# Shifted starts for the weights' slots and the row tiles of h in an fp32 kernel of two transformer blocks

## What is computed

```
for layer in 0, 1:
    h = modulate(rms_norm(x, g0), sh1, sc1)
    y = gmlp_mixer(h, ...)  if layer == 0  else  nsa_mixer(h, ...)
    x = x + g1 * rms_norm(y, g1n)
    h = modulate(rms_norm(x, g2), sh2, sc2)
    y = square(relu(h @ ff_w_in[layer])) @ ff_w_out[layer]      # 1024 -> 4096 -> 1024
    x = x + g2 * rms_norm(y, g3)
x = x + gt1 * rms_norm(token_mixers(modulate(rms_norm(x)) @ w_in) @ w_out)
u, gate = split(modulate(rms_norm(x)) @ w_up, 2)                # 1024 -> 2 x 2816
x = x + gt2 * rms_norm((silu(dwconv_grid(u)) * gate) @ w_down)
```

## Time and profile before

| | |
|---|---|
| median of 3 runs | 1018.43 us (1018.09 to 1018.6) |
| span of the profiled execution | 1018.0 us |
| TensorE busy | 994.2 us (98%), 6901 matmuls |
| weight loads busy | 877.0 us (86%), beside the matmuls |
| VectorE busy | 802.1 us (79%) |
| ScalarE busy | 539.3 us (53%) |
| from HBM | 239.37 MB, 236 GB/s over the span |

### The profile page before, as it was taken

One profiled execution on the slowest core, in us unless ns is written; L12 is line 12 of the kernel. 1 busy time (PEld: TensorE's weight loads), 2 busy tenths in 40 slices (PEclk: granted clock), 3 DMA queues, 4 the chain that ended last, 5 costly groups with the idle time before them and its releaser, 6 DMA issues.

```text
span 1018.0 us, 16927 instructions
## 1 busy us (share of the span) xinstructions
PE 994.2 (98%) x6901; PEld 877.0 (86%) x6901; DVE 802.1 (79%) x1208; ACT 539.3 (53%) x706; POOL 76.1 (7%) x80
## 2 busy tenths in 40 slices
PE   6999999999999999999999999999999999999997
PEld 3687799989987999887889999988999789999996
DVE  2459799868988987867978878872789799878796
ACT  4354644345446557766545454465764765454544
POOL 0000000000000000000630000000790000000000
PEclk9999999999999999999999999999999999999999
DMA  9999699969997998002999777725434286555511
GB/s 340 386 386 366 227 336 397 334 235 364 328 343 261 281 375 319 2 2 85 393 348 310 269 279 284 250 80 165 126 125 151 99 288 209 195 177 194 179 42 42
DMA packets 130333, 243.60 MB, mean 239 GB/s; under 512 B 6587, under 2 KB 95312, under 8 KB 124112
## 3 DMA queue, kind: packets, MB, share of 16 engines
q1 hardware_dynamic: 125616, 238.77, 66.6%
q10 hardware_dynamic: 4639, 3.76, 1.3%
HBM read 239.37 MB, written 1.05 MB: 236 GB/s over the span
## 4 chain that ended last, share of the span: by engine, by line
PE 85%; DVE 6%; DMA 3%; ACT 2%; issue 2%; SPq 2%; DVEq 0%; ACTq 0%
PE bank L2038 26%; PE bank L1970 13%; PE bank L1971 13%; PE bank L1972 13%; PE bank L2050 3%; DMA raw<-in_a_w_in_dram 1%; SPq L653 1%; DVE wlo L1198 1%; PE bank L2323 1%; DMA raw<-in_b_w_in_dram 1%; PE bank L2349 1%; PE bank L1864 1%; PE bank L2519 1%; DVE hcat L1338 1%; PE bank L2361 1%
## 5 line engine op out<-in xcount | busy, mean ns | idle before, releaser
L1198 DVE TENSOR_TENSOR wlo<-raw,whi 128x2048 fp32r<-128x2048 f32 x143 | 328.6, 2304 | 49.9 <-ACT whi L723 48.1
L723 ACT ACTIVATE whi<-raw 128x2048 fp32r<-128x2048 f32 x144 | 274.1, 1904 | 146.0 <-PE bank L2038 76.1
L1970 PE MATMUL bank<-hcat,whi 128*128 128x256 f32 x1096 | 312.1, 285 | 1.0 <-DVE wlo L1198 0.9
L1971 PE MATMUL bank<-hcat,whi 128*128 128x256 f32 x1096 | 310.1, 283 | 0.0
L1972 PE MATMUL bank<-hcat,wlo 128*128 128x256 f32 x1096 | 310.1, 283 | 0.0
L1970 PEld LDWEIGHTS bank<-hcat,whi 128*128 128x128 f32 x1096 | 210.1, 192 | 7.6 <-issue 3.0
L1971 PEld LDWEIGHTS bank<-hcat,whi 128*128 128x128 f32 x1096 | 210.2, 192 | 1.4
L1972 PEld LDWEIGHTS bank<-hcat,wlo 128*128 128x128 f32 x1096 | 210.1, 192 | 0.0
L1817 DVE SCALAR_TENSOR_TENSOR cvt<-ut,vec,cvt 128x189 f32<-128x189 f32 (+2 forms) x176 | 68.2, 429 | 20.9 <-ACT cvt L1161 18.4
L2038 PE MATMUL bank<-whi,fhi 128*128 128x512 f32 x240 | 75.0, 394 | 0.0
L2038 PE MATMUL bank<-wlo,fhi 128*128 128x512 f32 x240 | 74.1, 390 | 0.0
(11 more groups left out here) (432 smaller groups left out, 1631.1 us busy)
## 6 DMA issues: line engine op xcount, KB each, us to landing
raw<-in_ada_w_dram SPq DMA_DIRECT2D x40, 1024.0 KB, 8.6
raw<-in_ff_w_in_dram SPq DMA_DIRECT2D x32, 1024.0 KB, 7.4
raw<-in_ff_w_out_dram SPq DMA_DIRECT2D x32, 1024.0 KB, 7.1
raw<-in_w_ada_dram SPq DMA_DIRECT2D x24, 1024.0 KB, 6.4
raw<-in_w_up_dram SPq DMA_DIRECT2D x22, 1024.0 KB, 5.1
raw<-in_w_in_dram SPq DMA_DIRECT2D x12, 1024.0 KB, 5.4
raw<-in_w_down_dram SPq DMA_DIRECT2D x11, 1024.0 KB, 4.8
raw<-in_ada_w_dram SPq DMA_DIRECT2D x16, 512.0 KB, 12.1
```

The costliest lines, as they stand in the source:

```text
L723: act.activation(whi[:, m % SPL, 0:w], raw[:, pl.nm[m] % RAW, 0:w], ACT.Copy).then_inc(s_hi, 1)
L1198: dve.tensor_tensor(wlo[:, m % SPL, 0:w], raw[:, pl.nm[m] % RAW, 0:w], whi[:, m % SPL, 0:w], ALU.subtract).then_inc(s_lo, 1)
L1970: pe.matmul(dst, wh[:, kt, n], ah[:, kt, :], start=kt == 0, stop=False)
L1971: pe.matmul(dst, wh[:, kt, n], al[:, kt, :], start=False, stop=False)
```

## The change

The slots of `whi` and `wlo` become 20 values (80 bytes) longer, so they stand 8,272 bytes apart. The row tiles of `hcat` become 8 values (32 bytes) longer, 2,080 bytes apart; within one the high and the low part stay 1,024 bytes apart. The values between are not used. The last region starts at the next multiple of 128 bytes from `whi`, not of 512. By the allocation `wlo` starts 256 bytes later than before, `hcat` 512, `gcat`, the small buffers and the last region 768 (193,664 becomes 194,432). `raw` and `whi` stay. The instructions, their order and their waits are the same on every engine.

```
+W_SHIFT, H_SHIFT = 20, 8
...
-    whi = sb("whi", [P, SPL, CH], F32R)
-    wlo = sb("wlo", [P, SPL, CH], F32R)
+    whi = sb("whi", [P, SPL, CH + W_SHIFT], F32R)
+    wlo = sb("wlo", [P, SPL, CH + W_SHIFT], F32R)
     x = sb("x", [P, 2, D])
-    hcat = sb("hcat", [P, KT, 2, T], F32R)
+    hcat = sb("hcat", [P, KT, 2 * T + H_SHIFT], F32R)[:, :, 0:2 * T].rearrange("p k (a t) -> p k a t", a=2)
...
-    oP = whi_at + (at[0] - whi_at + 511) // 512 * 512
+    oP = whi_at + (at[0] - whi_at + 127) // 128 * 128
```

## The result

The changed kernel takes 1020.63 us (median of 14 runs) where the kernel before takes 1018.63 beside it (14 runs). The ratio of the times is **1.0016, with a 95% interval of 1.0009 to 1.0023**: the forecast gain of 0.9% didn't come, and 0.16% is lost. The profiled execution of after spans 1019.6 us, that of before 1018.0.

The account below looks back on a forecast made before the run. The prediction took TensorE's matmul stream (98% busy) to bound the kernel. 7.2 us less from the 256-column and 1.6 from the 512-column products gave 8.8 us less, 1018.4 to 1009.6 us (0.9% less), range 992 to 1019.5.

Parts of the forecast that it names:

- What bounds the kernel, and that only the two spacings count: Feed-forward blocks: TensorE is filled, so only start-to-start spacings of 120 ns (256 columns) and 227.9 ns (512) set their length.
- rival 4: First feed-forward block: the loads take its gain, 2.4 us are lost, giving 1012.0 us; chance 0.06.
- That the price depends on addresses: Compression products with shifted starts average 117.55 ns, aligned products of the same form 120 ns, so 2.45 ns less.
- Rival 1: All matmuls: addresses don't matter, the compression products' unevenness has another source; same time, 1018.4 us; chance 0.14.
- The 256-column products: Lines 1970 to 1972 in filled stretches: 2,928 matmuls, each 2.45 ns quicker, 7.2 us less.
- The 512-column products: Line 2038: 645 of 968 change phase with slots 1 and 2, each 2.45 ns quicker, 1.6 us less.
- upper bound of 2.0: Line 2038 at worst: the unsettled 230 ns spacing at the start, 2.1 x 968 = 2.0 us more.
- 13 to 14 ns: Loss per 256- or 512-column matmul against one column per cycle, read as the price of a 128-column fp32 weight load.
- Rival 3: Feed-forward blocks: one of three slots meets a bad phase, 10 ns on a third of 2,928, 9.8 us, 1028.2 us; chance 0.12.
- Rival 2: Each matmul falls to the quickest pairs seen, 27.3 us less, 991.1 us; chance 0.16.
- Writes into shifted slots and the region: ScalarE's and VectorE's writes into shifted slots, and the region moved as a whole: nothing at the end, 0 us.
- The signs that were named: Profile after: uneven 256-column steps near 117.5 ns, 24 of line 2038 in 5.40 to 5.47 us, first feed-forward round about 11.06.

Follow-up runs that it names:

- e1: Only the row tiles of `hcat` lengthened by 32 bytes, slots and region as in the kernel before; ratio to before 0.9972.
- e2: Only the slots of `whi` and `wlo` lengthened by 80 bytes, `hcat` and region as in the kernel before; ratio to before 1.0045.
- e3: Nothing lengthened, only the last region starts 256 bytes further than in the kernel before; ratio to before 0.9999.
- e5: Nothing lengthened, the whole of `hcat` moved by 192 bytes against the weights of the kernel before; ratio to before 0.9927, 1012.8 us.
- e9: Against the kernel before, everything from `whi` on moved by 192 bytes and `hcat` another 192; ratio to before 0.9915, 1010.71 us.
- e8: Against the kernel before, everything from `whi` on moved by 192 bytes, all distances as before; ratio to before 1.0001.
- e4: Against the kernel before, slots 64 bytes longer and the second buffers of `chi` and `clo` 16 bytes further; ratio to before 1.0002.
- e7: Against the kernel before, slots 32 bytes longer, `whi` and `wlo` moved by 32 bytes, `hcat` by 96; one execution, 1018.47 us beside 1018.9.
- e10: Against the kernel before, only `hcat` as a whole moved, by 64 bytes; ratio to before 0.996.
- e6: Against the kernel before, slots 32 bytes longer, `whi` and `wlo` moved by 160 bytes, `hcat` by 128; one execution, 1016.72 us beside 1018.9.

## Why the prediction was wrong, step by step

**What bounds the kernel, and that only the two spacings count: right for the feed-forward blocks.** No stage shows a new wait, VectorE's rows and the loads are as before, and the loads took nothing (rival 4): the first block runs at 329 and 330 GB/s.

**That the price depends on addresses: right.** Rival 1 has the time nearly right, but its reason is refuted: e1 gains 0.28% and e2 loses 0.45% by addresses alone. That after looks like "no effect" is a sum of two effects, and that rival 1 comes near is luck.

**The 256-column products: the right sign, the size too large.** The step that failed is "I take their mean, 117.55 ns". After has 118.5 in the first block, 1.3 ns less than before, and 118.3 in the last, 1.6 less (before, 863.40 - 846.42 = 16.98 us with a group of 5.47 left 119.9). With 1.3 for the 640 x 3 = 1,920 up to 810 us and 1.6 for the 336 x 3 = 1,008 behind the earlier trace rows that is 2.5 + 1.6 = 4.1 us instead of 7.2. The mechanism holds and the size was off. The compression products advance by 240 bytes from step to step and these by 32, so they run over other distances, and the table shows 116.7 to 120 by distance; a mean over one set of them isn't the mean over another.

**The 512-column products: the wrong sign.** The step that failed is "I give them the same 2.45 ns, as the price per weight load is the same". Three rounds take 16.61 us in their groups instead of 3 x 5.47 = 16.41, so the 720 of the first two layers (30 groups) lose 10 x 0.20 = 2.0 us; the 248 of the last block (10.3 groups) lose 10.3 x 0.15 = 1.5. That is 3.5 us more where 1.6 less was forecast, and above its upper bound of 2.0: the 230 ns of the earlier trace rows was taken as the worst, and slot 2 has 234. (The outgoing tile of the last block is in slot 2 in every round, so 480 + 248 = 728 of these products change their distance, not two in three, 645. And the two losses that were read as the same, "13 to 14 ns", are 13.3 and 14.6 by the prediction's own rows.) The kernel before has its 512-column products at the best distance of the table, and the prediction didn't ask whether the even 227.9 ns was already good.

The two errors, 3.1 and 5.1 us, are most of the distance between the 8.8 us forecast as a gain and the 1.6 us (0.16%) measured as a loss. By these two terms after would still be 0.6 us ahead.

**The products over `hcat`: a term that the prediction didn't have.** Its sum has `hcat` as the moving operand alone, and ahead of 130 us it counted no more than a possible gain. As stationary operand under 512 columns of weights `hcat` and `gcat` serve 407 steps, which lose 1.9 us: most of the 2 us or so that the two terms leave. Either shift alone does it: in the trace of e1, where only `hcat` is lengthened, these steps lose 1.6 us, and in e2's, where only the slots are, 1.5. So e1's gain would be larger without them. What is left, the 0.9 us in steps of over 0.3 us, is no more than single executions differ by (-1.0 in e3), and stays open.

**Rival 3** had the mechanism and the wrong place: "one of three slots meets such a phase all the time". It does, and two of the three, but in the 512-column products, and the 256-column ones stay under 120, by which the prediction took it as excluded. It was priced at 9.8 us on the wrong products and without the gain of the others beside it; it also stood there as all or nothing, so no case of the prediction held a gain on one form and a loss on the other. **Rival 2**, each matmul at the quickest steps, was far off: no distance of the table is below 116.7. A single tile can come near it (48 steps of 113.3 ns on average from 131 us on in e5), but no kernel keeps that pace through a block.

**Writes into shifted slots and the region: right.** 2,307 against 2,304 ns, and e3 at 0.9999.

**The signs that were named:** the uneven steps came, with 118.5 instead of 117.5 ns; the group of 24 was to be 5.40 to 5.47 and became 5.45 to 5.62; the round was to be 11.06 and stayed at 11.22. That last one would have looked like "nothing happened" without the group beside it.

## What to carry to other kernels

Where TensorE is full, the spacing from start to start is the unit of cost, and it has to be measured for each form of matmul by itself, for every product in which a moved buffer is read, as moving or as stationary operand: a price per weight load, seen on one form, did not even keep its sign on the other. A shift is better tried as one fixed distance for one kind of product (`hcat` alone by 192 bytes, 0.9927) than as a length that changes the distances of all products at once. And a time that doesn't change is not yet an edit without effect: undo the parts one at a time.

## What the runs showed of the hardware

- The pace of an fp32 matmul with 128 columns of weights loaded beside it follows the distance between its moving tile and the tile that is loaded, and doesn't change where both move by 192 bytes: 119.8 ns at 0 and 117.7 at 192 for 256 columns with the same 117.7 at two places (e5, e9), 119.8 at two places (before, e8).
- For 512 columns the distance of 0, and the pair of 112 and 240 in the last block of e4, give 227 ns; 80 gives 230.8 and 160 gives 234.2. Buffers sixteen bytes apart (e4, 5.63 against 5.45 us for 24) differ by 3%.
- At a distance of 0 the 256-column steps of before are an even 0.12 us; in after, at a mixture, one of 0.13 stands among steps with a mean of 0.118.
- The pace is not fixed by the distance alone: in e7's last block the same distances give 117.8 and 115.1 ns in alternate rounds. And the first seven steps of a 512-column group depend on what ran ahead of it (1,590 to 1,622 ns), where the other 17 take 226.7 each (before, e5, e10).
- Whether VectorE and ScalarE are at work beside them makes no difference to these steps (120.0 and 120.0 ns in before, 117.8 and 117.7 in e5).
- Open: why one distance gives different paces in different kernels, blocks and rounds (64: 229.6 and 233.3; 192 and 224 together 115.9 in e6's last block, but 117.7 and 118.1 in its first; the two of e7), and what the conflict is. The runs vary starts alone and show only how the pace follows.
